# Prompt logits as 128-row fp32r products: query parts stacked on the partitions, keys split in high and low

## The reference, cut to what matters

```python
kk, vv = with_prev(kb), with_prev(vb)          # block of 128 keys and the block before it (zeros before the first)
logits = jnp.einsum('nbqkgd,nbskd->nbkgqs', qb, kk) * (HEAD_DIM ** -0.5)
band = (rel >= 0) & (rel < WINDOW)             # WINDOW = 128
real = (jnp.arange(nb)[:, None] > 0) | (kpos >= ATTN_BLOCK)
p = sink_softmax(logits, valid, sinks)
out = jnp.einsum('nbkgqs,nbskd->nbqkgd', p, vv)
```

## Time and profile before

| what | value |
|---|---|
| median of three runs | 1264.87 us (1264.17 to 1265.15) |
| span of the profiled execution | 1265.4 us |
| TensorE busy | 1227.0 us (97%) |
| VectorE busy | 497.9 us (39%) |
| ScalarE busy | 306.3 us (24%) |
| GpSimd busy | 159.8 us (13%) |
| HBM over the span | 254 GB/s |

### The profile page before, as it was taken

One profiled execution on the slowest core, in us unless ns is written; L12 is line 12 of the kernel. 1 busy time (PEld: TensorE's weight loads), 2 busy tenths in 40 slices (PEclk: granted clock), 3 DMA queues, 4 the chain that ended last, 5 costly groups with the idle time before them and its releaser, 6 DMA issues.

```text
span 1265.4 us, 23325 instructions
## 1 busy us (share of the span) xinstructions
PE 1227.0 (97%) x8776; PEld 974.0 (77%) x8777; DVE 497.9 (39%) x1103; ACT 306.3 (24%) x560; POOL 159.8 (13%) x228
## 2 busy tenths in 40 slices
PE   7999999999999999999899999999999999999977
PEld 7988879999999999998899666556555566666643
DVE  4456574423453433566886112112112221111137
ACT  4344453322221222316012111111111111111121
POOL 0200000000000000004336121111111121211100
PEclk9999999999999999999999999999999999999999
DMA  9312122322223232606337999999999999999986
GB/s 279 103 37 67 34 68 51 80 71 79 89 68 100 67 109 76 211 21 208 141 115 305 420 419 419 421 421 419 420 421 419 420 421 418 420 421 421 421 351 264
DMA packets 98656, 307.31 MB, mean 243 GB/s; under 512 B 11244, under 2 KB 62404, under 8 KB 72840
## 3 DMA queue, kind: packets, MB, share of 16 engines
q1 hardware_dynamic: 85332, 275.20, 56.2%
q0 software_dynamic: 12304, 28.60, 5.8%
q10 hardware_dynamic: 948, 2.50, 0.6%
HBM read 294.45 MB, written 26.94 MB: 254 GB/s over the span
## 4 chain that ended last, share of the span: by engine, by line
PE 55%; DMA 37%; DVE 5%; issue 1%; DVEq 1%; ACT 0%; SPq 0%; POOL 0%; ACTq 0%; POOLq 0%
DMA w_exp<-in_w_e_down_dram 35%; PE proj L1051 32%; PE proj L1243 4%; PE proj L1384 3%; PE att L1454 2%; PE proj L1473 2%; PE att L1165 2%; PE att L1127 1%; DMA fold<-expert_rows 1%; PE att L1252 1%; PE proj L1338 1%; PE att L1178 1%; PE proj L1368 1%; PE proj L1077 1%; DVE res L2124 1%
## 5 line engine op out<-in xcount | busy, mean ns | idle before, releaser
L1454 PE MATMUL att<-w_exp,xt 128*64 128x256 f32 x2560 | 286.3, 380 | 2.7 <-DMA w_exp<-in_w_e_up_dram 2.1
L1454 PEld LDWEIGHTS att<-w_exp,xt 128*64 128x64 f32 x2560 | 207.6, 137 | 90.2 <-issue 27.5
L1051 PE MATMUL proj<-h_hi,w_hi 128*128 128x288 f32 x768 | 171.1, 304 | 0.0
L1051 PE MATMUL proj<-h_hi,w_lo 128*128 128x288 f32 x768 | 164.2, 295 | 0.0
L1051 PE MATMUL proj<-h_lo,w_hi 128*128 128x288 f32 x768 | 164.0, 295 | 0.0
L1473 PE MATMUL proj<-w_exp,ht_e 128*64 128x512 f32 x640 | 146.1, 597 | 9.6 <-DMA w_exp<-in_w_e_down_dram 4.9
L1051 PEld LDWEIGHTS proj<-h_hi,w_hi 128*128 128x128 f32 x768 | 122.0, 188 | 16.2 <-issue 15.2
L1051 PEld LDWEIGHTS proj<-h_lo,w_hi 128*128 128x128 f32 x768 | 123.5, 188 | 0.0
L1051 PEld LDWEIGHTS proj<-h_hi,w_lo 128*128 128x128 f32 x768 | 123.4, 188 | 0.0
L468 DVE TENSOR_TENSOR w_lo<-w_raw,w_hi 128x2048 fp32r<-128x2048 f32 x33 | 75.6, 2291 | 91.9 <-ACT w_hi L458 86.8
L1473 PEld LDWEIGHTS proj<-w_exp,ht_e 128*64 128x64 f32 x640 | 50.4, 136 | 77.7 <-issue 76.0
(11 more groups left out here) (384 smaller groups left out, 1810.8 us busy)
## 6 DMA issues: line engine op xcount, KB each, us to landing
w_exp<-in_w_e_gate_dram SPq DMA_DIRECT2D x64, 1024.0 KB, 16.9
w_exp<-in_w_e_up_dram SPq DMA_DIRECT2D x64, 1024.0 KB, 17.0
w_exp<-in_w_e_down_dram SPq DMA_DIRECT2D x64, 1024.0 KB, 17.1
w_raw<-in_w_in_dram SPq DMA_DIRECT2D x21, 1024.0 KB
part<-expert_rows SPq DMA_DIRECT2D x8, 1536.0 KB, 21.2
w_raw<-in_w_in_dram SPq DMA_DIRECT2D x8, 512.0 KB
w_raw<-in_w_attn_out_dram SPq DMA_DIRECT2D x8, 512.0 KB
w_raw<-in_w_conv_out_dram SPq DMA_DIRECT2D x4, 1024.0 KB
```

The lines of the kernel that those rows point to most:

```text
L1051: last = nc.tensor.matmul(proj[:, 2 * i + a, 0:HALF], lhs, x[:, c, a * HALF:(a + 1) * HALF], start=(c == 0 and n == 0), stop=(c == KC - 1 ...
L1454: last = nc.tensor.matmul(att[e * SLOT:(e + 1) * SLOT, m, 0:FF], xt[:, c, e * SLOT:(e + 1) * SLOT], weights[e][:, c, :], start=(c == 0), s ...
```

## The change

The prompt logits are computed by fp32r matmuls over all 128 rows. For each head the stationary operand `q_both` holds the high part of the query on partitions 0 to 63 and the low part on 64 to 127. The moving operand is the key, its high part on both halves of the partitions (`k_hi`) and then its low part on both (`k_lo`), accumulated in the same PSUM columns. ScalarE writes the high parts of keys and queries, VectorE the low ones, and the slot of a query group is now freed by VectorE for both halves. `query` is called per slot: on ScalarE in iterations 2 and 4 (10 and 12, 18 and 20), on VectorE in 3 and 4 (11 and 12, 19 and 20). The first block uses keys 0 to 255 with a causal mask in place of 128 zero keys, so the zero blocks and their two memsets on GpSimd go. `k_hi` takes the place of the cached values, whose load moves from group 3 on SyncE's queue to behind the last prompt logits (`lg_ready`).

```diff
...
-        q_t = at("q_t", [P, NPAIR_H, T], F32, o_b)
+        q_both = at("q_both", [P, 2, 2, 2, T], F32R, o_b)
...
+        k_hi = at("k_hi", [P, 2, SEQ], F32R, o_f + 14336)
+        k_lo = at("k_lo", [P, 2, SEQ], F32R, o_d + 6 * 4 * T)
... SyncE
-                if n == 3:
-                    sp.dma_start(cache_v[:, :, :], win_v[0].rearrange("b w g d -> w b (g d)")).then_inc(ld_cv, 16)
...
             for n in range(2):
                 load(Step(G_CONV[n]), w_in, (COL_CC, COL_CH)[n])
+            sp.wait_ge(lg_ready, N_STEP)
+            sp.dma_start(cache_v[:, :, :], win_v[0].rearrange("b w g d -> w b (g d)")).then_inc(ld_cv, 16)
... GpSimd
-            nc.gpsimd.memset(k_t[:, 0:WIN], 0.0).then_inc(zeroed, 1)
-            nc.gpsimd.memset(v_tok[:, 0, :], 0.0).then_inc(zeroed, 1)
... ScalarE
+            act.drain()
+            for e in range(2):
+                r = slice(e * HD, (e + 1) * HD)
+                for h in range(2):
+                    last = nc.scalar.activation(k_hi[h * HD:(h + 1) * HD, e, :], k_t[r, 0:SEQ], ACT.Copy)
+            last.then_inc(qk_hi, 1)
+
+            def query(j, i):
+
+                act.wait_ge(mm_ready[i], Q_AT[j] + 1)
+                if j >= 2:
+                    act.wait_ge(lg_ready, 8 * (j - 1))
+                for e in range(2):
+                    last = nc.scalar.activation(two(q_both[0:HD, j % 2, i, e, :]), slot(i)[e * HD:(e + 1) * HD], ACT.Copy,
+                                                scale=HD ** -0.5)
+                last.then_inc(qk_hi, 1)
...
                 if n in (2, 10, 18):
-                    query(n // 8 + 1)
+                    query(n // 8 + 1, 0)
+                if n in (4, 12, 20):
+                    query(n // 8 + 1, 1)
... TensorE
+                    c0 = (max(blk, 1) - 1) * P
                     for e in range(2):
-                        r = slice(e * HD, (e + 1) * HD)
-                        last = nc.tensor.matmul(att[:, e, 0:2 * P], q_t[r, pair, blk * P:(blk + 1) * P],
-                                                k_t[r, blk * P:blk * P + 2 * P], start=True, stop=True)
+                        for k in (k_hi, k_lo):
+                            last = nc.tensor.matmul(att[:, e, 0:2 * P], q_both[:, j % 2, n % 2, e, blk * P:(blk + 1) * P],
+                                                    k[:, e, c0:c0 + 2 * P], start=(k is k_hi), stop=(k is k_lo))
... VectorE
+            def query(j, i):
+
+                dve.wait_ge(qk_hi, 2 * j + i + 2)
+                m = 2 * j + i
+                last = nc.vector.tensor_scalar(
+                    q_smp[:, :, m * S_S:(m + 1) * S_S],
+                    proj[:, 2 * i + 1, SEQ - HALF:HALF].rearrange("p (b s) -> p b s", b=NB_S), HD ** -0.5, None, ALU.mult)
+                if m == NPAIR_H - 1:
                     last.then_inc(qs_ready, 1)
+                for e in range(2):
+                    last = nc.vector.scalar_tensor_tensor(
+                        two(q_both[HD:P, j % 2, i, e, :]), slot(i)[e * HD:(e + 1) * HD], HD ** -0.5,
+                        two(q_both[0:HD, j % 2, i, e, :]).bitcast(F32), ALU.mult, ALU.subtract)
+                last.then_inc(mm_free[i], 1)
...
             split_lo(dve, Step(2))
+            dve.wait_ge(qk_hi, 1)
+            for e in range(2):
+                r = slice(e * HD, (e + 1) * HD)
+                for h in range(2):
+                    nc.vector.tensor_tensor(k_lo[h * HD:(h + 1) * HD, e, :], k_t[r, 0:SEQ], k_hi[r, e, :].bitcast(F32),
+                                            ALU.subtract)
+            query(0, 0)
             dve.wait_ge(tr_kv, 1)
...
-            query(0)
+            query(0, 1)
...
+                if n in (3, 11, 19):
+                    query(n // 8 + 1, 0)
                 if n in (4, 12, 20):
-                    query(n // 8 + 1)
+                    query(n // 8 + 1, 1)
...
```

More of the change, by code:

```diff
@@ L74, in pack_constants @@
     ident = np.eye(P, dtype=np.float32)
-    q, k = np.arange(P)[:, None] + P, np.arange(2 * P)[None]
-    band = (q - k >= 0) & (q - k < WIN)
-    first = band & (k >= P)
+    row, k = np.arange(P)[:, None], np.arange(2 * P)[None]
+    band = (row + P - k >= 0) & (row + P - k < WIN)
+    first = k <= row
     mask_p = np.where(np.stack([first, band], 1), 0.0, neg).astype(np.float32).reshape(P, -1)
@@ L149, in decoder_step @@
         smp = at("smp", [P, KC, 2, NS], F32R, 20480)
-        k_t = at("k_t", [P, WIN + T], F32, o_e)
-        v_tok = at("v_tok", [P, 1 + NT, P], F32, o_e + 2816)
+        k_t = at("k_t", [P, T], F32, o_e)
+        v_tok = at("v_tok", [P, NT, P], F32, o_e + 2816)
         v_t = at("v_t", [P, T], F32, o_e + 5888)
@@ L229, in decoder_step @@
         mm_free = [sem(f"mm_free{i}") for i in range(2)]
-        zeroed = sem("zeroed")
+        qk_hi = sem("qk_hi")
         tr_x, x_hi, x_lo = sem("tr_x"), sem("x_hi"), sem("x_lo")
@@ L676, in _ @@
         def _(pool):
-            nc.gpsimd.memset(k_t[:, 0:WIN], 0.0).then_inc(zeroed, 1)
-            nc.gpsimd.memset(v_tok[:, 0, :], 0.0).then_inc(zeroed, 1)
             pool.wait_ge(kv_tok_ready, 1)
             pool.dma_start(nk_p[0, 0].rearrange("w g d -> w (g d)"), k_tok[:, 0, :]).then_inc(st_out, 16)
-            pool.dma_start(nv_p[0, 0].rearrange("w g d -> w (g d)"), v_tok[:, NT - 1, :]).then_inc(st_out, 16)
+            pool.dma_start(nv_p[0, 0].rearrange("w g d -> w (g d)"), v_tok[:, NT - 2, :]).then_inc(st_out, 16)
             for b in range(NB_S):
@@ L685, in _ @@
                 pool.dma_start(nv_s[0, b, WIN - S_S:WIN].rearrange("w g d -> w (g d)"),
-                               v_tok[b * S_S:(b + 1) * S_S, NT, :]).then_inc(st_out, 16)
+                               v_tok[b * S_S:(b + 1) * S_S, NT - 1, :]).then_inc(st_out, 16)
             pool.wait_ge(cn_out, 1)
@@ L800, in _ @@
             act.wait_ge(mm_ready[0], 1)
[L801 to L806, removed]
+            nc.scalar.activation(two(k_t[:, :]), slot(0), ACT.Copy).then_inc(mm_free[0], 1)
+            act.drain()
[12 more added lines that the diff above has]
+                last.then_inc(qk_hi, 1)
             def gate_row(j):
@@ L1101, in _ @@
                 nc.tensor.transpose(att[0:w, t // 4, t % 4 * P:(t % 4 + 1) * P], v_t[:, t * P:t * P + w], ident[:, :])
-            nc.tensor.transpose(att[:, 1, P:2 * P], k_t[:, WIN + SEQ - P:WIN + SEQ], ident[:, :])
-            nc.tensor.transpose(att[0:NS, 1, 2 * P:3 * P], k_t[:, WIN + SEQ:], ident[:, :])
+            nc.tensor.transpose(att[:, 1, P:2 * P], k_t[:, SEQ - P:SEQ], ident[:, :])
+            nc.tensor.transpose(att[0:NS, 1, 2 * P:3 * P], k_t[:, SEQ:T], ident[:, :])
             for b in range(NB_S):
@@ L1126, in weighted @@
                         r = slice(e * HD, (e + 1) * HD)
-                        last = nc.tensor.matmul(att[r, 3, 0:256], v_tok[:, blk + c, r],
+                        last = nc.tensor.matmul(att[r, 3, 0:256], v_tok[:, max(blk, 1) - 1 + c, r],
                                                 p_t[:, c, e, b % 2 * 2:b % 2 * 2 + 2, :].rearrange("p m q -> p (m q)"),
@@ L1136, in _ @@
             nc.tensor.transpose(att[:, 2, P:P + 24], cwraw[:, :], ident[0:24, 0:24]).then_inc(tr_conv, 1)
-            pe.wait_ge(zeroed, 2)
             pe.wait_ge(kv_tok_ready, 1)
@@ L1153, in _ @@
                         nc.tensor.matmul(o[:, 0:WIN], q_smp[r, b, :], cache_kt[r, b, :], start=True, stop=True)
-                        last = nc.tensor.matmul(o[:, WIN:KEYS_S], q_smp[r, b, :], k_t[r, WIN + SEQ:], start=True, stop=True)
+                        last = nc.tensor.matmul(o[:, WIN:KEYS_S], q_smp[r, b, :], k_t[r, SEQ:T], start=True, stop=True)
                     last.then_inc(sl_ready, 1)
@@ L1206, in _ @@
                 nc.tensor.matmul(o, cache_v[:, b, :], ps_t[:, b, :], start=True, stop=False)
-                last = nc.tensor.matmul(o, v_tok[0:NS, NT, :], psn_t[:, b, :], start=False, stop=True)
+                last = nc.tensor.matmul(o, v_tok[0:NS, NT - 1, :], psn_t[:, b, :], start=False, stop=True)
                 if b == NB_S - 1:
@@ L1572, in _ @@
             nc.vector.tensor_copy(two(v_t[:, :]), slot(1)).then_inc(mm_free[1], 1)
[L1573 to L1582, removed]
-                    last.then_inc(qs_ready, 1)
+            def query(j, i):
[5 more added lines that the diff above has]
+                if m == NPAIR_H - 1:
+                    last.then_inc(qs_ready, 1)
+                for e in range(2):
[3 more added lines that the diff above has]
+                last.then_inc(mm_free[i], 1)
             def gate_row(j):
@@ L1590, in _ @@
             split_lo(dve, Step(2))
+            dve.wait_ge(qk_hi, 1)
[4 more added lines that the diff above has]
+                                            ALU.subtract)
+            query(0, 0)
             dve.wait_ge(tr_kv, 1)
-            nc.vector.tensor_copy(v_tok[:, 1:NT, :].rearrange("p a n -> p (a n)"), att[:, 0, :])
-            nc.vector.tensor_copy(v_tok[0:NS, NT, :], att[0:NS, 1, 0:P])
```

(4 more changed lines are left out.)

## The result

The changed kernel takes 1269.72 us (median of 6, 1267.96 to 1272.22) where the kernel before takes 1265.01: ratio 1.0036, interval 1.0026 to 1.0046. It is slower by 4.7 us, above the forecast of 1264.0 and above the range's end of 1268.0. Its profiled execution has a span of 1269.2 us. A timed execution is some 1.8 us longer than its span (1271.06 for this one), so the profiled execution of the kernel before, with 1265.4, stands for about 1267.2: the longest of that kernel's six, not one 0.5 above their median. The two spans are therefore only 3.8 us apart. Behind a wait of 3.41 us in the routing (near 630 us) that execution has 6.8 us at half clock, this one 3.4.

What follows compares the result with a forecast made beforehand. It took TensorE to bound the kernel, a microsecond in the attention loop being one at the end. Logits -8.4, last eight steps -0.7 and queries +8.2 gave -0.9 us, so 1264.0 us, range 1260.5 to 1268.0.

Steps and rivals of the forecast that it cites:

- The logits: First 24 attention steps: a prompt logits group falls from 0.83 to 0.48 us on TensorE, saving 8.4 us.
- The last eight steps: Attention steps with thin filling, about every second bounded by VectorE: new logits save 0.7 us, bounds 0 and 2.8.
- The queries: VectorE frees accumulator 0 later, so TensorE waits before the first logits and at steps 4, 12, 20: 8.2 us lost.
- The restart: TensorE after each new wait at steps 4, 12 and 20: 0.1 us more for weights that load unhidden.
- The covers: Key copies and subtractions, first query work, moved cached-values load and loads queued behind it fit idle time: costed at nothing.
- The clock: Rival, slower: TensorE's clock falls in the new waits, 1.7 us a fall; chance of one 0.2, of more 0.12.
- the forecast case: Whole kernel: the three terms sum to -0.9 us without clock falls, 1264.0 us, called no change; chance 0.36.

Runs made afterwards that it cites:

- the doubled group: Kernel before the change with every prompt logits group issued twice, the second writing the same numbers again: 1278.95 us, ratio 1.0102.
- the last kernel: Changed kernel with query handover one iteration earlier, done head by head, and a filling chunk moved from behind the loop into step 29: 1257.53 us, ratio 0.9932.
- the one with the wait added: Kernel before the change, old logits kept, with ScalarE copying accumulator 0's queries in iterations 3, 11, 19 instead of 2, 10, 18: 1271.35 us, ratio 1.0042.
- the kernel with half the products: Changed kernel without the products with the keys' low parts, two products a step instead of four: 1258.76 us, ratio 0.995.

## Why the prediction was wrong

*The logits.* 0.48 us a group was forecast, 0.47 measured; 0.83 before. Right. The reason was right as well: the doubled group shows 0.40 us that come once a group.

*The last eight steps.* From step 23 to 31 the logits' starts lie 26.5 us apart, before 27.2. That is 0.7 us, but half of it (0.35) is the group of step 23, which the 8.4 holds already; the last eight steps themselves give some 0.3. The two short waits behind them grew from 0.16 and 0.26 us to 0.34 and 0.63, 0.55 in all where I had allowed 0.1. So this term, forecast at 0.7, came to about nothing.

*The queries.* 2.1 us of idle time for steps 12 and 20, measured 2.12 and 2.12. Step 4: 2.9 forecast, 2.41 measured. TensorE reached the head of step 4 at 60.65, not at 59.9, and VectorE was done at 62.9, near the 62.7. The restart, for which I had 0.1 us and no row, is 0.25. So the three waits cost 2.66 + 2.37 + 2.37 = 7.4 us from start to start, the 7.4 of the forecast, in part because two misses offset. The first logits came 1.2 us later in one profile and 0.55 in the other, forecast 0.8; in both 3.71 us lie between TensorE's last pair of query products and them where it was 2.81, so 0.9, and the rest is when that pair came. VectorE's subtraction takes 0.756 us where I had scaled 0.82 from a row. The mechanism, its engine and its sizes were right.

*The covers.* Key copies, the moved load and what is queued behind it cost nothing. Right.

*The clock.* This is the step that failed. The place was right, the 3.4 us were right, and "it decides the sign from the second fall" was right. The price was near: 1.7 us forecast, 1.5 measured, since TensorE's products start 1.8 and not 2 times as far apart. The chance was not. The forecast has no fall, and I gave 0.2 to one and 0.12 to more. By my own rows at least one was to be expected: step 4's wait was forecast at 2.9 us, above the 2.31 of the kernel before that pulled the clock. For the two of 2.1 I took that 2.31 as the least that does, but one wait that did and one of 1.30 that didn't set no limit between them. The profiled executions of all these kernels show how it goes in the attention stage:

| TensorE idle | waits seen | followed by half clock |
|---|---|---|
| 0.8 to 1.5 us | 11 | 0 |
| 1.6 to 1.9 us | 7 | 1 |
| 2.1 us | 6 | 3 |
| 2.4 to 2.6 us | 3 | 3 |

(Eleven: the start's 0.83 to 0.85 us in five executions, step 30's 0.86 in the last kernel and 0.85 in the one with doubled logits, 1.30 in the kernel before and in the one with the wait added, and that one's two of 1.48. Seven: step 30's 1.63 to 1.65 in five executions and 1.91 in the kernel with half the products, and the 1.88. Six: the changed kernel twice and the one with half the products. Three: step 4 of the same three.) The bounds of these classes lie where the waits happened to fall, and the counts are small. By this table the changed kernel has about two falls an execution at its three new waits, 3.0 us; the comparison with TensorE kept busy gives 4.6, and the intervals of the two kernels leave about 2 us of room either way. Without the falls the change is the tie that was forecast. With them it is a loss of 0.36%. The 0.7 us of the last eight steps are too few to show in it.

In the prediction's terms: the forecast case and the clock rival belonged together, since the waits that I was sure of (-8.4 - 0.7 + 8.2) were the rival's condition. A sum that leaves 2 us waits on TensorE has to price them at 2 us and the clock's share, here 1.5 us times the chance of a fall each.

## What to carry to other kernels

When a tuned loop has one engine that never waits, an edit that shortens its work and gives another engine more hands the deadline to that engine; follow each buffer's release through that engine's own queue, since there the order decides, not the busy share. A wait of 2 us on TensorE cost up to 1.5 us more than itself here, so a change that brings both a gain and such a wait should be made together with the reordering that removes it: here moving one job one iteration forward turned +0.34% into -0.39%. Small matrix products in another tile form inside a stream of full ones should be priced with the two switches; here these were half of their cost.

## What the runs showed of the hardware

- A wait of TensorE of about 2.1 us was followed by 3.4 us at 1.2 GHz in 3 of 6 cases, waits of 1.63 to 1.91 us in 1 of 7, and waits of 2.41 to 2.63 us in all three. The half clock costs 1.5 us of those 3.4. The Trainium skill (TensorE: Matmul & The Clock Gate, Part 1) ties the half clock to an idle engine and says that the point of transition differs between runs of one kernel; the traces agree that executions differ, here in whether the clock falls at all behind one and the same wait. In the first profile of the changed kernel it falls 0.7 and 0.35 us after TensorE has started again at the first two waits, and with the start itself at the third.
- Seventeen useless products of 128 rows by 256 columns in each of three such waits kept the clock up and made the kernel 4.6 us faster.
- Two heads as 64-row fp32 products side by side stream in 0.43 us, four fp32r products of 128 rows in 0.47: for a contraction of 64 the full-height form brings no faster streaming, only no switches (0.40 us a group). Fp32 transposes over all 128 rows in the same stream lose nothing on the way in and out (0.43 us for four).
- VectorE's subtraction with a product read on one half of the partitions and its result on the other took 0.756 us for 576 columns, no more than a plain one.
